# Layer norm of a convolution, taken two channel groups at a time

## The reference, cut to what matters

```python
def _layer_norm(x, g, b):
    mu = jnp.mean(xf, axis=-1, keepdims=True)
    xc = xf - mu
    y = xc * lax.rsqrt(jnp.mean(xc * xc, axis=-1, keepdims=True) + EPS)
    return y * g + b

    conv = jax.nn.silu(_layer_norm(y, ln_g, ln_b))      # y: the depthwise convolution
    mixed = concatenate([_rms_norm(attn, ...), _rms_norm(conv, conv_out_norm[i])])
    h = h + mixed @ w_out[i]
    h = h + 0.5 * _swiglu_ffn(_rms_norm(h, ffn2_norm[i]), ...)
```

## Time and profile before

| | |
|---|---|
| median of 3 runs | 1449.06 us (1448.72 to 1449.65) |
| profiled execution, its own time | 1449.12 us |
| span of the profiled execution | 1446.9 us |
| mean granted TensorE clock | 0.998 of full |
| PE busy | 1422.6 us, 98% |
| DVE busy | 892.0 us, 62% |
| ACT busy | 803.8 us, 56% |

### The profile page before, as it was taken

One profiled execution on the slowest core, in us unless ns is written; L12 is line 12 of the kernel. 1 busy time (PEld: TensorE's weight loads), 2 busy tenths in 40 slices (PEclk: granted clock), 3 DMA queues, 4 the chain that ended last, 5 costly groups with the idle time before them and its releaser, 6 DMA issues.

```text
span 1446.9 us, 20576 instructions
## 1 busy us (share of the span) xinstructions
PE 1422.6 (98%) x7680; PEld 1173.6 (81%) x7680; DVE 892.0 (62%) x1218; ACT 803.8 (56%) x1242; POOL 11.1 (1%) x20
## 2 busy tenths in 40 slices
PE   9999999999999999999899999999999999999997
PEld 7778888888888888888688888888888886888886
DVE  5976766665655556556865565655565668655555
ACT  7688664654356444466765444564444667544444
POOL 1000000000000000000000000000000000000000
PEclk9999999999999999999999999999999999999999
DMA  8563355655566665552366656566655424666560
GB/s 299 158 212 115 117 175 184 199 181 178 189 186 205 187 186 178 162 166 102 117 203 181 185 176 213 176 189 185 184 182 161 159 90 131 205 188 181 189 197 29
DMA packets 132778, 249.57 MB, mean 172 GB/s; under 512 B 8616, under 2 KB 16128, under 8 KB 132704
## 3 DMA queue, kind: packets, MB, share of 16 engines
q1 hardware_dynamic: 131264, 244.70, 54.6%
q0 software_dynamic: 1088, 3.54, 0.8%
q10 hardware_dynamic: 352, 0.32, 0.1%
HBM read 247.48 MB, written 1.05 MB: 172 GB/s over the span
## 4 chain that ended last, share of the span: by engine, by line
PE 91%; DVE 4%; ACT 3%; issue 1%; DMA 0%; ACTq 0%; DVEq 0%
PE acc L2152 27%; PE acc L2154 27%; PE acc L2153 27%; PE turn L2165 5%; DVE w_lo L1292 2%; PE turn L2214 1%; PE pair L2567 1%; ACT w_hi L682 1%; PE pair L2193 1%; ACT u_t L1188 0%; PE pair L2187 0%; PE turn L2277 0%; PE pair L2222 0%; DVE taps L1824 0%; ACT x_hi L755 0%
## 5 line engine op out<-in xcount | busy, mean ns | idle before, releaser
L1292 DVE TENSOR_TENSOR w_lo<-stage,w_hi 128x1024 fp32r<-128x1024 f32 (+2 forms) x480 | 562.7, 1184 | 373.7 <-ACT w_hi L682 368.3
L682 ACT ACTIVATE w_hi<-stage 128x1024 fp32r<-128x1024 f32 (+2 forms) x480 | 487.4, 1029 | 449.4 <-PE acc L2154 446.9
L2152 PE MATMUL acc<-w_hi,x_hi 128*128 128x512 f32 (+2 forms) x1280 | 506.7, 396 | 3.3 <-DVE w_lo L1292 2.8
L2154 PE MATMUL acc<-w_hi,x_lo 128*128 128x512 f32 (+2 forms) x1280 | 494.5, 386 | 0.0
L2153 PE MATMUL acc<-w_lo,x_hi 128*128 128x512 f32 (+2 forms) x1280 | 493.9, 386 | 0.0
L2152 PEld LDWEIGHTS acc<-w_hi,x_hi 128*128 128x128 f32 x1280 | 240.6, 188 | 54.0 <-issue 7.1
L2154 PEld LDWEIGHTS acc<-w_hi,x_lo 128*128 128x128 f32 x1280 | 240.5, 188 | 50.1
L2153 PEld LDWEIGHTS acc<-w_lo,x_hi 128*128 128x128 f32 x1280 | 240.9, 188 | 44.9 <-issue 0.2
L2152 PE MATMUL acc<-w_hi,g_hi 128*128 128x512 f32 x352 | 137.7, 391 | 0.0
L2153 PE MATMUL acc<-w_lo,g_hi 128*128 128x512 f32 x352 | 137.1, 389 | 0.0
L2154 PE MATMUL acc<-w_hi,g_lo 128*128 128x512 f32 x352 | 137.0, 389 | 0.0
(11 more groups left out here) (334 smaller groups left out, 1163.7 us busy)
## 6 DMA issues: line engine op xcount, KB each, us to landing
stage<-in_ffn_w_gate_up SPq DMA_DIRECT2D x176, 512.0 KB, 3.7
stage<-in_ffn_w_down SPq DMA_DIRECT2D x88, 512.0 KB, 4.5
stage<-in_w_in SPq DMA_DIRECT2D x64, 512.0 KB, 4.3
stage<-in_w_ff SPq DMA_DIRECT2D x64, 512.0 KB, 4.3
stage<-in_w_out SPq DMA_DIRECT2D x16, 512.0 KB, 3.9
stage<-in_w_ple_gate SPq DMA_DIRECT2D x16, 512.0 KB, 4.5
stage<-in_w_lru_up SPq DMA_DIRECT2D x8, 512.0 KB, 4.6
stage<-in_w_o SPq DMA_DIRECT2D x8, 512.0 KB, 4.3
```

The lines of the kernel that those rows point to most:

```text
L682: act.activation(w_hi[:, n.slot(SPLIT), 0:t, 0:w], stage[:, n.slot(STAGE), 0:t, 0:w], ACT.Copy).then_inc(hi_done, 1)
L1292: dve.tensor_tensor(w_lo[:, n.slot(SPLIT), 0:t, 0:w], stage[:, n.slot(STAGE), 0:t, 0:w], w_hi[:, n.slot(SPLIT), 0:t, 0:w].bitcast(F32), AL ...
L2152: pe.matmul(dst, xh, wh, start=kt == 0, stop=False)
L2154: mm = pe.matmul(dst, xl, wh, start=False, stop=kt == last)
```

## The change

The four groups are handled as two halves of two groups. Sums: each half has a sum of its own (`group_sums`, 128x2x256), and PE adds the halves by accumulating two products for each mean. Centring, squares and the product with the reciprocal root are two instructions each, with a semaphore count for each half (`s_centred` is new). The first feature mean is asked for in `ready` of k-tile 2 of `Lout_a0` in place of k-tile 1, and the second in that of k-tile 0 of `Lout_a1` in place of k-tile 3 of `Lout_a0`. Three one-element activations (`warm`) put the loads of the Sqrt, Silu and Sqrt tables ahead of the waits or splits that they stood behind or beside. The first unit of `Lout_c1` is split by ACT ahead of `embedding_squares(1)`, and by DVE ahead of the last sums; `rms_boundary` then starts from unit 1. The diff, cut to its core:

```diff
-                wait(act, score_free, SCORES.at("Lsum", 1, layer))
-                act.activation(ysq[:, :, :], y[:, :, :], ACT.Square).then_inc(s_ysq, 1)
+                def group_squares(half, ready, count):
+                    wait(act, ready, count)
+                    pair_of = slice(2 * half, 2 * half + 2)
+                    act.activation(ysq[:, pair_of, :], y[:, pair_of, :], ACT.Square).then_inc(s_ysq, 1)
+                for half in range(2):
+                    group_squares(half, s_centred, Count(half + 1, [(layer, 2)]))
+                act.activation(warm(1), eps, ACT.Sqrt)
                 wait(act, score_done, SCORES.at("Lsum", 2, layer))
                 act.activation(sig[:, 0, 0:S], score[:, 0:S], ACT.Sqrt, bias=eps).then_inc(score_free, 1)
...
                 act.activation(rows, rows, ACT.Sqrt, bias=eps).then_inc(s_rattn, 1)
+                act.activation(warm(2), eps, ACT.Silu)
                 split("Lout_c0", layer, units=[0])
...
+                silu_rows(0)
+                silu_rows(1)
+                rows_hi(0)
+                rows_hi(1)
+                silu_rows(2)
+                split("Lout_c0", layer, units=[1])
+                silu_rows(3)
+                rows_hi(2)
+                group_squares(0, s_silu, Count(2, [(layer, KC)]))
+                rows_hi(3)
+                group_squares(1, s_silu, Count(4, [(layer, KC)]))
+                split("Lout_c1", layer, units=[0])
                 embedding_squares(1)
+                act.activation(warm(3), eps, ACT.Sqrt)
                 wait(act, score_done, SCORES.at("Lsum", 3, layer))
...
-                rms_boundary("Lout_c1", "Lb_norm", ..., "Lb_up0", "Lout_c", layer)
+                rms_boundary("Lout_c1", "Lb_norm", ..., "Lb_up0", "Lout_c", layer, 1)
@@ DVE
-                def sum_groups(src):
-                    link(dve.tensor_tensor(two_groups, src[:, 0:2, :], src[:, 2:4, :], ALU.add))
-                    dve.tensor_tensor(group_sum, two_groups[:, 0, :], two_groups[:, 1, :], ALU.add).then_inc(s_group_sum, 1)
+                def sum_groups(src, half):
+                    dve.tensor_tensor(group_sums[:, half, :], src[:, 2 * half, :], src[:, 2 * half + 1, :],
+                                      ALU.add).then_inc(s_group_sum, 1)
                 wait(dve, s_yin, Count(2, [(layer, 2)]))
-                sum_groups(y)
+                for half in range(2):
+                    sum_groups(y, half)
                 wait(dve, score_done, SCORES.at("Lsum", 1, layer))
+                for half in range(2):
+                    yh = y[:, 2 * half:2 * half + 2, :]
+                    dve.scalar_tensor_tensor(yh, score[:, 0:S].unsqueeze(1).to_broadcast(over), -1.0, yh,
+                                             ALU.mult, ALU.add).then_inc(s_centred, 1)
                 split("Lout_a1", layer, units=range(1, 2))
+                wait(dve, s_centred, Count(2, [(layer, 2)]))
+                dve.sem_inc(score_free, 1)
+                for half in range(2):
+                    wait(dve, s_ysq, Count(half + 1, [(layer, 4)]))
+                    sum_groups(ysq, half)
                 wait(dve, score_free, SCORES.at("Lsum", 2, layer))
                 link(dve.reciprocal(rs, rs))
-                dve.tensor_tensor(y[:, :, :], y[:, :, :], rs.unsqueeze(1).to_broadcast(over), ALU.mult).then_inc(s_yn, 1)
+                for half in range(2):
+                    yh = y[:, 2 * half:2 * half + 2, :]
+                    dve.tensor_tensor(yh, yh, rs.unsqueeze(1).to_broadcast(over), ALU.mult).then_inc(s_yn, 1)
...
                 add_residual("Lout_a1", 1, stat[:, at:at + TT], layer)
-                wait(dve, s_ysq, Count(2, [(layer, 2)]))
-                sum_groups(ysq)
+                split("Lout_c1", layer, units=[0])
+                for half in range(2):
+                    wait(dve, s_ysq, Count(2 + half + 1, [(layer, 4)]))
+                    sum_groups(ysq, half)
@@ PE
                 def feature_means(i):
-                    wait(pe, s_group_sum, Count(i + 1, [(layer, 3)]))
                     free(SCORES, score_free, "Lsum", i, layer)
-                    pe.matmul(score[:, 0:S], mean, group_sum, start=True, stop=True).then_inc(score_done, 1)
+                    for half in range(2):
+                        wait(pe, s_group_sum, Count(2 * i + half + 1, [(layer, 6)]))
+                        mm = pe.matmul(score[:, 0:S], mean, group_sums[:, half, :], start=half == 0, stop=half == 1)
+                    mm.then_inc(score_done, 1)
                 def squares_mean(kt):
-                    if kt in (1, 3):
-                        feature_means(kt // 2)
+                    if kt == 2:
+                        feature_means(0)
                 chunk("Lout_a0", x_hi, x_lo, layer, ready=squares_mean)
-                chunk("Lout_a1", x_hi, x_lo, layer)
+                chunk("Lout_a1", x_hi, x_lo, layer, ready=lambda kt: feature_means(1) if kt == 0 else None)
                 def row_means(kt):
                     wait(pe, s_convlo, Count(kt + 1, [(layer, KC)]))
                     if kt == 3:
-                        wait(pe, s_group_sum, Count(3, [(layer, 3)]))
+                        wait(pe, s_group_sum, Count(6, [(layer, 6)]))
                         for t in range(TT):
-                            mm = pe.matmul(score[:, t:t + 1], group_sum[:, t * P:(t + 1) * P], mean[:, 0:1], start=True, stop=True)
+                            for half in range(2):
+                                mm = pe.matmul(score[:, t:t + 1], group_sums[:, half, t * P:(t + 1) * P], mean[:, 0:1],
+                                               start=half == 0, stop=half == 1)
```

More of the change, by code:

```diff
@@ L80 @@
 NV2 = 44
-STATS = dict(rstd=0, attn=TT, ple=2 * TT, e=4 * TT, half=5 * TT, q=7 * TT, conv=8 * TT, warm=9 * TT, last=10 * TT)
-C_STATS = 13 * TT
+STATS = dict(rstd=0, attn=TT, ple=2 * TT, e=4 * TT, half=5 * TT, q=7 * TT, conv=8 * TT, warm=9 * TT, last=11 * TT)
+C_STATS = 14 * TT
 C_ID, C_EPS, C_M1, C_M2, C_ROPE, C_ROPEC, C_CMASK, C_ROWOK, C_INV, C_SEL, C_SELM, C_END = np.cumsum(
@@ L478, in build @@
         s_yn = sem("s_yn")
+        s_centred = sem("s_centred")
         s_silu = sem("s_silu")
@@ L712, in rows_scaled, with rms_boundary @@
                 return ins
-            def rms_boundary(last, norm, dst, gain, first, residual, layer=None):
+            def rms_boundary(last, norm, dst, gain, first, residual, layer=None, done=0):
                 n_last, a = N_UNITS[last], min(3, N_UNITS[last] // 2)
-                split(last, layer, units=range(min(n_last, a + 3)))
+                split(last, layer, units=range(done, min(n_last, a + 3)))
                 early = 1 if n_last < SPLIT else 0
@@ L1213, in _, with silu_rows, rows_hi @@
                 act.activation(rows, rows, ACT.Sqrt, bias=eps).then_inc(s_rattn, 1)
+                act.activation(warm(2), eps, ACT.Silu)
                 split("Lout_c0", layer, units=[0])
[L1215 to L1226, removed]
+                def silu_rows(n):
+                    wait(act, s_yn, Count(n // 2 + 1, [(layer, 2)]))
+                    act.activation(y[:, n, :], y[:, n, :], ACT.Silu, scale=vec2[:, layer, V2["ln_g"] + n:V2["ln_g"] + n + 1],
+                                   bias=vec2[:, layer, V2["ln_b"] + n:V2["ln_b"] + n + 1]).then_inc(s_silu, 1)
+                def rows_hi(n):
+                    wait(act, s_silu, Count(n + 1, [(layer, KC)]))
+                    act.activation(x_hi[:, 4 + n, :], y[:, n, :], ACT.Copy,
+                                   scale=vec2[:, layer, V2["conv"] + n:V2["conv"] + n + 1]).then_inc(s_convhi, 1)
+                silu_rows(0)
[10 more added lines that the diff above has]
+                split("Lout_c1", layer, units=[0])
                 embedding_squares(1)
+                act.activation(warm(3), eps, ACT.Sqrt)
                 wait(act, score_done, SCORES.at("Lsum", 3, layer))
@@ L1312, in row_factors, with rms_boundary @@
                 wait(dve, s_rstd, RSTD.at(name, 1, layer))
-            def rms_boundary(parts, norm, hi, lo, gain, first, layer=None, at=None, before=lambda: None):
+            def rms_boundary(parts, norm, hi, lo, gain, first, layer=None, at=None, before=lambda: None, done=0):
                 n_last, a = N_UNITS[parts[1]], min(3, N_UNITS[parts[1]] // 2)
@@ L1319, in rms_boundary @@
                     scale = stat[:, STATS[at]:STATS[at] + TT]
-                split(parts[1], layer, units=range(min(n_last, 3)))
+                split(parts[1], layer, units=range(done, min(n_last, 3)))
                 before()
@@ L1999, in _ @@
                 wait(dve, s_yin, Count(2, [(layer, 2)]))
-                sum_groups(y)
-                rs = sig[:, 0, 0:S]
-                over = [P, KC, S]
-                wait(dve, score_done, SCORES.at("Lsum", 1, layer))
-                dve.scalar_tensor_tensor(y[:, :, :], score[:, 0:S].unsqueeze(1).to_broadcast(over), -1.0, y[:, :, :],
```

(3 more changed lines are left out.)

18 lines of the change are left out of this document (10 added, 8 removed).

## The result

The changed kernel takes 1451.74 us (median of 20 runs, 1451.07 to 1453.77) against 1448.97 us (20 runs, 1448.22 to 1449.65): ratio 1.0023, 95% interval 1.0016 to 1.0029. It is slower by 2.8 us, and the interval leaves no doubt about the sign. I had said 1450.7 us and "no change that can be told", with slower at 0.16. The time lies in the range. It lies at the border that I drew at 0.2%: a little past it by the ratio, a little short of it by the medians (2.77 us of 2.9).

What follows compares the result with a forecast made beforehand. PE, busy 98% of the span, was taken as the bound; the DVE and ACT chain's steps summed to +0.8 us a layer, +1.6 in two, on 1449.12: 1450.7 us, "same" (chance 0.68), eight times in ten 1446.6 to 1452.9.

Steps and rivals of the forecast that it cites:

- 1 first mean: First mean in `Lout_a0`, asked for at k-tile 2: PE's wait of 0.71 us goes, mean 0.67 later for the chain.
- step 2: Centring after the first mean: two products in place of one add 0.43 us; delay 1.10, or 0.1 less with weights loaded.
- 4 second mean: Second mean at k-tile 0 of `Lout_a1`: starts 0.39 us later; PE waits 0.34 in place of 1.00.
- Step 6: Reciprocal, product and first split of `Lout_c0`: DVE's split at 707.95 against 707.06, ACT's slack 0.5 us; Sqrt load stays hidden.
- 7 wait at `Lout_c0`: Start of `Lout_c0`: 0.89 us later, PE's wait growing from 0.33 to about 1.75.
- 8 last sums: Last sums on DVE, behind the early split of `Lout_c1` (1.13 us more, halves save 0.38): end at 716.85 against 715.19.
- Step 9: Row means at k-tile 3 of `Lout_c0`: PE waits 1.45 us (before 0.69), k-tile 3 starts 2.09 later.
- 10 wait at `Lout_c1`: Start of `Lout_c1`: the wait of 1.32 us is gone, the start 0.77 later.
- 11 stage longer by: Transposes two k-tiles into `Lout_c1`: residual of `Lout_c0` just in time, 0 to 0.3 us late at worst; sum +0.8 a layer.
- three signs of being wrong: First group's `x_lo` ending ahead of 710.2, row means starting ahead of 715.5, or ACT's `w_hi` of `Lout_c0` later than 708.
- the table load that holds ACT: Rival: Silu load ahead of the first `Lout_c0` split holds ACT, slip 0.9 us a layer, 1452.5 us; chance 0.16.
- PE's waits really go: Rival: DVE and ACT chain some 2.5 us shorter, 2.8 us a layer won, 1443.6 us; chance 0.16.

Runs made afterwards that it cites:

- e8: Changed kernel with the two half sums joined by a third add on DVE and one product for each mean; 1452.16 us.
- e2_no_warm: Changed kernel without its three `warm` activations; 1452.11 us.
- e5: Changed kernel with DVE's last group sums ahead of the residual of `Lout_a1` and the early split of `Lout_c1`; 1447.34 us.
- e7: Kernel before, whole groups, with last sums ahead of the residual of `Lout_a1`, early split of `Lout_c1`, and ACT's second embedding squares moved later; 1445.29 us.
- e9: Changed kernel with its two means asked for at k-tiles 1 and 3 of `Lout_a0`, as before the change; 1448.30 us.
- e4: Kernel before with only the early split of the first unit of `Lout_c1` on ACT and DVE; 1451.09 us.
- e3: Changed kernel with the first unit of `Lout_c1` split at its old, later place on ACT and DVE; 1450.72 us.
- e11: e7 with 10 dummy one-column matmuls (20 records) a layer ahead of `Lout_c1`; 1450.29 us.
- e12: e7 with 20 dummy transposes of 128 columns a layer ahead of `Lout_c1`; 1449.09 us.
- e1: Changed kernel with 7 dummy transposes ahead of `Lout_c0` and 6 ahead of the wait for the last sums; 1450.66 us.

## Why the prediction was right, and what it lacked

Each step against the trace of the changed kernel. Times are counted from the first matmul of `Lout_a0` (696.18 before, 695.85 after), and "later" is against the kernel before:

| step | forecast | measured |
|---|---|---|
| 1 first mean, no wait, later by | 0.67 | 0.64 |
| 2 centring later by | 1.10 | 0.96 |
| 4 second mean: wait, later by | 0.34, 0.39 | 0.33, 0.30 |
| 5 root later by | 0.82 | 0.71 |
| 6 DVE's split of `Lout_c0` later by | 0.89 | 0.78 |
| 6 slack of ACT's split | 0.5 | 0.58 |
| 7 wait at `Lout_c0`, later by | 1.75, 0.89 | 1.75, 0.77 |
| 8 last sums end later by | 1.66 | 1.52 |
| 9 wait at the row means | 1.45 | 1.45 |
| 10 wait at `Lout_c1` | none | none |
| 11 stage longer by, at full clock | 0.8 | 0.65 |
| clock of TensorE | no term | 1.5 in a slow stretch |

None of the three signs of being wrong came: the first `x_lo` pair starts at 710.20 and ends at 711.08, the row means start at 716.48, and ACT has `w_hi` of `Lout_c0` at 706.93.

**The chain was right in each link, and in sign.** The one term that was off is in step 2. There I had named 0.1 less, for the case that the mean's weights are already in the array, and did not take it. The 0.1 came: with no idle ahead of it, the first mean reaches DVE 1.06 us after its start, and in e8, with one product and no idle either, 0.63 us after it (698.88 to 699.51). So one product takes 0.63 in place of 0.74, and the second 0.43 as I had it. That the weights are the reason is not shown. That is most of the 0.15 by which the chain came out shorter than the sum; no other link is off by more than a few hundredths. One reading was too bold: layer 1 does not repeat layer 0 "to the hundredth". Before the change PE waits 0.80 us for the first mean there and 0.73 for the row means, against 0.71 and 0.69, and the stage is 0.07 longer. It does not move the sum, since what counts is the difference that the change makes.

**Step 6 was right that the table loads are nothing.** e2_no_warm settles it, and the rows of ACT above show the `warm` activation starting 1.30 and 1.29 us behind the start of its load. The Trainium skill ("ScalarE: Activation LUTs", What ACT_TABLE_LOAD costs) puts a drain of 1.38 us behind the load; in these rows there is none, so the slip that this rule would have made did not come, and the slack stayed at 0.58. That rival, the table load that holds ACT, is refuted as a mechanism, though the outcome "slower" that it stood for came from elsewhere.

**What the sum lacked is a term for the clock.** Step 9 forecast a wait of 1.45 us ahead of the row means and 0.43 more of row means, which made these twice as long, and I read both as time only. Together they are 2.3 us in which PE streams next to no columns, and after them TensorE ran at 1.2 GHz for some 3.4 us. 2 x 0.65 for the chain and 1.5 for one stretch give 1448.97 + 2.8 = 1451.8; measured 1451.74. The forecast 1450.7 missed 1.0 of it: 1.5 not foreseen, less the chain's 2 x 0.15 over-priced, and 0.2 that is noise between the medians. So it was partly luck that the time fell inside the range, and inside the likeliest case's own range of 1449.7 to 1452.1: both had been drawn for other terms, and a run with two stretches (1453.0 and more) lies outside both. The trace of before could have warned me only in part. It shows 0.69 + 0.44 us at this place and no fall, and I did not ask what 1.45 + 0.88 would do.

**The rival "PE's waits really go"** failed for the reason given: the change moved waits rather than taking them. But it is the rival whose kernel exists. e5 and e7 show that the waits at the row means and at `Lout_c1` can both go, or all but go, by the order of work on DVE and ACT alone.

**What stays open.** In the nine slow stretches of these profiles the clock falls between just ahead of and 1.5 us behind the first chunk matmul after the one-column matmuls, and stays at half for 3.4 us each time. Why a slow stretch comes in some executions and layers and not in others of the same kernel (e9's layers wait 1.45 and 1.43 us, without and with one) is not settled; I can say which kernels show it and which do not in 8 to 20 runs, not when it falls. By their times each of the changed kernel's 20 runs has at least one such stretch, and only a part of e4's and e9's has; that is open too.

## What to carry to other kernels

When a wait of the bounding engine ends with a tiny operation on another engine, look at what that engine was given to do directly ahead of it: two sums of 0.4 us stood behind 2.6 us of work with slack, and swapping them was worth 1.45 us a layer where the halving was worth 0.4. A side product that is asked for later in the busy engine's order delays its whole chain; the wait that this takes away comes back where the chain ends. And a wait of TensorE has a second price: if it stands next to matmuls that stream few columns, count a possible stretch at half clock on top of it, and move the wait away from them if it can't be removed: in e3 PE waits as long in all as in the changed kernel, but mostly elsewhere, and e3 is 1.0 us faster.

## What the runs showed of the hardware that was not expected

- A granted clock of half for about 3.4 us can follow 2.3 us of waiting and one-column matmuls. It costs 1.5 us, since matmuls start 0.43 us apart in place of 0.23. Waits of 1.75 us and 1.3 us that stood between wide matmuls did not bring it about (e3, e5; no slow stretch in either profile, and none to be seen in the times of 22 runs).
- One-column matmuls leave PE busy in the profile and still let the clock fall (e11: busy 3.80 of 3.80 us, then 0.53), where transposes of 128 columns in as many records do not (e12). The Trainium skill ("TensorE: Matmul & The Clock Gate", Why this matters for your kernels) warns of idle gaps between bursts of matmuls; in this trace there was none, and the clock fell all the same.
- Short dummy transposes in a wait (e1: 0.93 and 0.82 us) kept the clock up, in the profile and by the times in 10 of 11 runs, although idle time of 0.80 and 0.57 us was left.
